# Attention on Trainium2: TensorE sends a tile's product with the values ahead of the next tile's scores and its transposes

## The reference, cut to what matters

```python
s_win = jnp.einsum('bhjqd,bhijkd->bhjqik', q_r, k_r) + bias        # window of 8 rows, masked
s_ctx = jnp.einsum('bhjqd,bhtd->bhjqt', q_r, k_ctx)                # 256 cached keys
p = jax.nn.softmax(jnp.concatenate([s_win, s_ctx], axis=-1), axis=-1)
o = jnp.einsum('bhjqik,bhijkd->bhjqd', p_win, v_r) + jnp.einsum('bhjqt,bhtd->bhjqd', p_ctx, v_ctx)
```

## Time and profile before

| | us |
|---|---|
| median of 3 runs | 3932.43 |
| lowest and highest | 3928.03, 3935.48 |
| the profiled execution's own time | 3931.9 |
| its span in the trace | 3930.1 |
| PE busy | 3514.1 |
| DVE busy | 2422.3 |
| ACT busy | 1935.5 |

### The profile page before, as it was taken

The page is one execution under the profiler, slowest core; times in us unless marked ns, Lnnn a source line. Parts: engine busy times, 40 slices in busy tenths (PEclk is TensorE's granted clock), DMA queues, the critical chain, the costliest instruction groups (busy, mean ns, idle before and its releaser), DMA issues.

```text
span 3930.1 us, 59373 instructions
## 1 busy us (share of the span) xinstructions
PE 3514.1 (89%) x23329; PEld 3175.1 (81%) x23329; DVE 2422.3 (62%) x3212; ACT 1935.5 (49%) x3195; POOL 849.2 (22%) x1106
## 2 busy tenths in 40 slices
PE   6798699989648839589999999999999999999997
PEld 2253478878546628489999999999999999999997
DVE  5445421137667852567776777777777767777766
ACT  1102311136412231156666666666666666666775
POOL 1102020011023303132232232223223222322321
PEclk7898899989769869689999999999999999999998
DMA  1443352244133334278888788888888888888885
GB/s 61 172 150 126 143 138 90 90 108 124 73 102 131 123 121 142 107 226 268 263 255 263 257 265 260 261 265 257 263 258 265 259 257 269 257 261 261 263 286 202
DMA packets 215934, 780.08 MB, mean 198 GB/s; under 512 B 28130, under 2 KB 30469, under 8 KB 211432
## 3 DMA queue, kind: packets, MB, share of 16 engines
q1 hardware_dynamic: 201112, 724.79, 55.8%
q0 software_dynamic: 14544, 51.50, 5.0%
HBM read 716.32 MB, written 59.88 MB: 197 GB/s over the span
## 4 chain that ended last, share of the span: by engine, by line
PE 56%; DVE 2%; ACT 0%; issue 0%; POOL 0%; DMA 0%; ACTq 0%; DVEq 0%; POOLq 0%
PE exp_ps L2133 25%; PE exp_py L2133 13%; PE exp_ps L2135 9%; PE exp_py L2135 5%; PE exp_ps L2132 2%; PE exp_ps L2116 0%; DVE exp_lo L126 0%; PE exp_py L2132 0%; PE exp_pr L2125 0%; PE exp_pp L2126 0%; DVE exp_idx L1706 0%; DVE exp_affT L1708 0%; DVE exp_val L1705 0%; DVE exp_xb L2050 0%; DMA exp_xp<-hidden_rows,exp_next_q 0%
## 5 line engine op out<-in xcount | busy, mean ns | idle before, releaser
L2133 PE MATMUL exp_ps<-exp_xt,exp_hi 128*128 128x320 f32 x5632 | 1444.7, 342 | 2.5 <-DVE exp_xt L2015 1.3
L126 DVE TENSOR_TENSOR exp_lo<-exp_raw,exp_hi 128x1024 fp32r<-128x1024 f32 x1056 | 1368.4, 1328 | 80.4 <-ACT exp_hi L122 77.4
L122 ACT ACTIVATE exp_hi<-exp_raw 128x1024 fp32r<-128x1024 f32 x1056 | 1117.8, 1059 | 424.9 <-PE exp_py L2135 231.0
L2135 PE MATMUL exp_ps<-exp_xt,exp_lo 128*128 128x160 f32 x4928 | 1163.4, 236 | 0.0
L2133 PEld LDWEIGHTS exp_ps<-exp_xt,exp_hi 128*128 128x128 f32 x5632 | 1009.7, 189 | 3.9 <-DVE exp_xt L2015 1.7
L2135 PEld LDWEIGHTS exp_ps<-exp_xt,exp_lo 128*128 128x128 f32 x4928 | 940.8, 191 | 0.0
L2133 PE MATMUL exp_py<-exp_hid,exp_hi 128*128 128x320 f32 x2816 | 757.3, 350 | 0.0
L2135 PE MATMUL exp_py<-exp_hid,exp_lo 128*128 128x160 f32 x2688 | 634.4, 236 | 0.0
L2133 PEld LDWEIGHTS exp_py<-exp_hid,exp_hi 128*128 128x128 f32 x2816 | 528.6, 188 | 1.2
L2135 PEld LDWEIGHTS exp_py<-exp_hid,exp_lo 128*128 128x128 f32 x2688 | 514.0, 191 | 0.0
L1884 POOL TENSOR_TENSOR exp_hd<-exp_sl,exp_s 128x160 f32<-128x160 f32 x352 | 285.1, 810 | 1026.4 <-ACT exp_sl L1983 1026.4
(11 more groups left out here) (466 smaller groups left out, 4719.6 us busy)
## 6 DMA issues: line engine op xcount, KB each, us to landing
exp_raw<-in_w SPq DMA_DIRECT2D x1056, 512.0 KB, 4.6
filts_wa<-in_w_ada SPq DMA_DIRECT2D x24, 1024.0 KB, 4.9
hys_raw<-in_basis_s SPq DMA_DIRECT2D x32, 512.0 KB, 3.9
features<-proj_xr SPq DMA_DIRECT2D x20, 640.0 KB, 3.5
proj_raw<-in_w_in SPq DMA_DIRECT2D x24, 512.0 KB, 4.8
filts_raw<-in_kbasis_s SPq DMA_DIRECT2D x18, 512.0 KB, 5.4
spectrum_s<-filts_spec SPq DMA_DIRECT2D x34, 256.0 KB, 2.0
hys_kt<-spectrum_s POOLq DMA_DIRECT2D x14, 512.0 KB, 4.0
```

The lines of the kernel that those rows point to most:

```text
L122: act.activation(self.hi[:, c % self.ns, :], self.raw[:, c % self.nr, :], ACT.Copy).then_inc(self.hi_done, 1)
L126: dve.tensor_tensor(self.lo[:, c % self.ns, :], self.raw[:, c % self.nr, :], self.hi[:, c % self.ns, :].bitcast(F32), ALU.subtract).then_i ...
L2133: mm = pe.matmul(out[:, 0:2 * CAP], wh, rhs, start=first, stop=last)
L2135: mm = pe.matmul(out[:, 0:CAP], wl, rhs[:, 0:CAP], start=False, stop=False)
```

## The change

In TensorE's loop `values(n - 1)` moves from the end of a pass to its beginning. The last product, `values(NT - 1)`, stays behind the loop. No instruction is added or removed, and no other engine's list is touched.

```diff
             scores(0)
             for n in range(NT):
+                if n:
+                    values(n - 1)
                 if n + 1 < NT:
                     scores(n + 1)
                 transposes(n)
-                if n:
-                    values(n - 1)
             values(NT - 1)
```

## The result

| | before | changed |
|---|---|---|
| median, us | 3930.4 (4 runs) | 4087.73 (4 runs, 4085.73 to 4088.86) |
| ratio to before | | 1.0398, 95% interval 1.038 to 1.0416 |

What follows compares the result with a forecast made beforehand. TensorE was taken to bound the attention. The ring adds 96.9 us at the high clock or 204.5 at the low; a mean clock of 0.60 gives 176.4 more on 3931.9, so 4108 us, range 4030 to 4145.

Steps and rivals of the forecast that it cites:

- The ring: Attention pass as scores, add_max, copy, norm, values, scores without overlap: 3.95 us per window tile at high clock, 5.47 low.
- two rows: Profiled stretches with like TensorE load: clock 0.56 at 58% busy (1070 to 1125 us), 0.71 at 64% (60 to 150).
- the likeliest one: Attention mostly at the low clock, mean 0.50 to 0.65: 4096 to 4136 us, chance 0.62.
- the one to which I gave 0.17: Attention clock alternating about evenly, mean 0.65 to 0.85; 4074 us at 0.75, chance 0.17.
- The product waits for the norm: In the attention, values(n) follows norm(n - 1) by 0.15 us; ScalarE's copy_win ends earlier, 1020.54 against 1021.32.
- The waits that leave: Attention waits for the exponentials, 14.7 us in all, 5.3 in one stall, and ScalarE's long one for head 1's keys, vanish.
- The clock: TensorE, busy 57% of an attention pass instead of 93%, is granted a mean clock of 0.60: 176.4 us more.
- the forecast's own sum: Attention's 7.9 heads at 36.56 us each at high clock and 50.18 at low, a fifth of time high: 369 us.
- The rival of a high clock: Attention clock stays above 0.85 since the gaps are short: 4029 us, up to 4054; chance 0.18.
- The rivals without a loss: Attention order closes TensorE's present waits (3917 us), or nothing happens because values waits for both anyway; 0.02 together.
- the point of balance: Attention gains only if copy and norm are ready within 0.19 us of the transposes' end; forecast wait 1.6 us.

Runs made afterwards that it cites:

- the run with filling: The changed kernel plus eight matmuls that nobody reads behind each tile's transposes, to keep TensorE busy: 4030.86 us, ratio 1.0252.
- the run with the norm first: The changed kernel with VectorE's pass in the order norm(n - 1), add_max(n + 1), copy_ctx(n): 4078.82 us, ratio 1.0363.

## Why the prediction was right

4087.7 us was measured against a forecast of 4108 in a range from 4030 to 4145. The ring was worked out and came true. That the time lies so near the forecast is in part luck, since the clock was a choice between two rows: by my own cases the measured time falls not in the likeliest one (clock 0.50 to 0.65, 4096 to 4136 us) but just beyond it, in the one to which I gave 0.17. I had also written that the prediction is wrong if the clock over the attention is above 0.65. It was 0.66, so by that mark the clock's part of it failed, narrowly.

- **The ring** was right for window tiles, link by link. Such a pass measures 3.94 to 3.95 us at the high clock, as forecast, and 5.54 against 5.47 at the low one, where the product takes 2.12 instead of 2.06. The passes that score a context tile behind a window tile's product measure 2.93 at the high clock, where my terms give 0.20 + 0.43 + 0.41 + 0.96 + 1.11 = 3.11. The two links from the last score matmul to the copy were read too long: the reduction at 870.15 stood behind a norm that VectorE was still at (869.95 + 0.28), and the copy starts before the reduction's own time is over. In the changed kernel they take 0.32 and 0.34 us instead of 0.43 and 0.41. So it is partly chance that the sum for 79 passes at the high clock, 289.4, is what the run with filling measured: the added matmuls put back some 4 us there.
- **The product waits for the norm**, not for the copy or for ScalarE: it comes 0.15 us behind the norm, and follows the copy once the norm is moved.
- **The waits that leave**, for the exponentials and most of the one for head 1's loads, did leave, and were in the difference.
- **The clock** is the main term that was mis-sized. I took a mean of 0.60 from stretches of other phases with a like load; it was 0.66. Then 0.32 of the time is at the high clock, and the forecast's own sum gives 7.9 / (0.32 / 36.56 + 0.68 / 50.18) = 354 us for the passes and 4093 for the kernel. The loop took 349.3 us, 4.9 less. A part of that must lie in how the clock's changes fall inside the passes, which a mean doesn't tell: the pass from 907.92 to 911.87 took 3.95 us although the clock fell to 0.50 at 909.8, when TensorE had nothing but transposes left, which are off the ring. No run gives the shares. The rest of the way from 4093 to the profiled execution's 4085.7 us is the start of the loop, 3.7 us earlier.
- **The rival of a high clock** was wrong. The rule of the Trainium skill that I gave for it (TensorE: Matmul & The Clock Gate, "Why this matters for your kernels", which warns of long idle gaps between bursts) would have given 4029. Here no wait of TensorE in the loop is longer than 1.9 us, and the trace has the clock falling from 1.00 to 0.50 fifteen times in the loop. So the measurement disagrees with what I took from that rule. I also wrote that no row has transposes alone. The trace of the kernel before has such a place outside the attention: 32 transposes and nothing else between 1158.44 and 1163.85 us, behind 31.80 us without a matmul, and the clock rose from 0.50 to 1.00 while they ran. So there transposes did bring the clock up, against what I had cited for the low one.
- **The rivals without a loss** fell too. TensorE waited 1.45 us for the norm in a high-clock pass, where 0.19 would have been the point of balance.

## What to carry to other kernels

In a software pipeline over in-order engines, look at what is queued behind the instruction that waits. Here the product waited for VectorE while the scores that VectorE needed next stood behind it. The two engines took turns, where VectorE's work had lain under TensorE's before; with the scores sent first, or with VectorE's copy ahead of its reductions, most of the loss is gone. And when an edit leaves TensorE with short idle times in every pass, cost it at both clock levels and read the granted clock over that loop, since a shorter wait can be paid back by a lower clock, as the run with the norm first shows.

## What the runs showed of the hardware

- Adding 640 matmuls to idle time made the kernel 57 us faster, since the granted clock over the loop went from 0.66 to 1.00.
- The clock did not simply follow TensorE's share of work in a pass. With the norm first the high-clock pass got shorter (3.49 us with the same 2.26 us of work, so 65% instead of 57%), and yet the clock over the loop was lower, 0.57 against 0.66. This version also varied most, from 4061.92 us with a clock of 0.910 over the whole span to 4093.04 us with 0.900. Why is left open.
- In the changed kernel the clock kept step with the heads. In heads 1 to 3 the passes measure 4.1 to 4.2 and 4.3 us, three times 5.54, twice 3.95, once 5.54, and twice 2.93. With the norm first the clock fell only 4 times in the profiled loop, and whole heads ran at 0.50.
- The step from VectorE's last write to TensorE's matmul was 0.15 us behind the norm, and 1004.23 - 1003.75 - 0.42 = 0.06 behind the copy.
